# Weight sums moved from GpSimd to VectorE, and a last quarter that begins four runs early, in a two-layer encoder

## What is computed

```python
for i in range(2):
    h = rms_norm(x, mix_norm[i])
    x = x + (neighbourhood_attention(h, ...) if i == 0 else sliding_window_gqa(h, ...))
    h = rms_norm(x, mlp_norm[i])
    x = x + square(relu(h @ mlp_w_in[i])) @ mlp_w_out[i]
return rms_norm(x, final_norm)
```

## Time and profile before

| | us |
|---|---|
| median of 3 runs | 1118.18 (1117.50 to 1118.21) |
| the profiled execution's own time | 1117.47 |
| its span, first to last instruction | 1115.8 |
| PE busy | 1091.5 (98%) |
| DVE busy | 885.5 (79%) |
| ACT busy | 596.0 (53%) |
| POOL busy | 272.7 (24%) |

### The profile page before, as it was taken

One profiled execution on the slowest core, in us unless ns is written; L12 is line 12 of the kernel. 1 busy time (PEld: TensorE's weight loads), 2 busy tenths in 40 slices (PEclk: granted clock), 3 DMA queues, 4 the chain that ended last, 5 costly groups with the idle time before them and its releaser, 6 DMA issues.

```text
span 1115.8 us, 18152 instructions
## 1 busy us (share of the span) xinstructions
PE 1091.5 (98%) x6524; PEld 961.5 (86%) x6524; DVE 885.5 (79%) x1432; ACT 596.0 (53%) x1020; POOL 272.7 (24%) x340
## 2 busy tenths in 40 slices
PE   8999999999999999999889999999999999999987
PEld 6888888888998998998887888888899899899786
DVE  7778887768958968968887799976895895895795
ACT  6777767555425425425444788845543542542553
POOL 6544332200210210210464244201020030020151
PEclk9999999999999999999999999999999999999999
DMA  6332322232332332332213233234313313313312
GB/s 213 115 91 78 108 79 75 88 121 94 114 114 76 113 114 76 114 114 71 100 58 105 56 97 100 71 104 132 124 48 133 124 46 133 119 53 132 101 51 76
DMA packets 37098, 109.65 MB, mean 98 GB/s; under 512 B 6480, under 2 KB 10864, under 8 KB 37024
## 3 DMA queue, kind: packets, MB, share of 16 engines
q1 hardware_dynamic: 32112, 100.74, 26.9%
q0 software_dynamic: 4768, 7.90, 2.9%
q10 hardware_dynamic: 144, 0.02, 0.0%
HBM read 105.93 MB, written 2.70 MB: 97 GB/s over the span
## 4 chain that ended last, share of the span: by engine, by line
PE 93%; DVE 3%; issue 1%; ACT 1%; POOL 0%; DMA 0%; DVEq 0%; POOLq 0%; ACTq 0%
PE acc L661 17%; PE acc L663 17%; PE acc L662 17%; PE pt_ps L661 4%; PE pt_ps L663 4%; PE pt_ps L662 4%; PE acc L695 3%; PE s_ps L661 3%; PE s_ps L663 3%; PE s_ps L662 3%; PE om_ps L661 2%; PE om_ps L662 2%; PE om_ps L663 2%; PE om_ps L987 2%; PE pt_ps L974 2%; PE om_ps L814 1%
## 5 line engine op out<-in xcount | busy, mean ns | idle before, releaser
L661 PE MATMUL acc<-h_hi,w_parts 128*128 128x512 f32 x736 | 291.3, 396 | 2.5 <-DVE w_parts L1473 2.0
L663 PE MATMUL acc<-h_hi,w_parts 128*128 128x512 f32 x736 | 286.8, 390 | 0.0
L662 PE MATMUL acc<-h_lo,w_parts 128*128 128x512 f32 x736 | 286.6, 389 | 0.0
L661 PEld LDWEIGHTS acc<-h_hi,w_parts 128*128 128x128 f32 x736 | 138.3, 188 | 33.1 <-DVE w_parts L1473 2.8
L663 PEld LDWEIGHTS acc<-h_hi,w_parts 128*128 128x128 f32 x736 | 138.1, 188 | 29.4
L662 PEld LDWEIGHTS acc<-h_lo,w_parts 128*128 128x128 f32 x736 | 138.4, 188 | 28.1 <-issue 0.7
L1267 ACT CAST w_parts<-w_raw 128x1024 fp32r<-128x1024 f32 x62 | 65.3, 1054 | 144.3 <-PE acc L663 120.8
L661 PE MATMUL pt_ps<-u_hi,w_parts 128*128 128x256 f32 x384 | 110.5, 288 | 5.7 <-DVE x_res L1741 3.5
L1293 ACT CAST w_parts<-room 128x1024 fp32r<-128x1024 f32 x64 | 66.0, 1046 | 87.9 <-DVE room L1695 67.4
L663 PE MATMUL pt_ps<-u_hi,w_parts 128*128 128x256 f32 x384 | 109.4, 285 | 0.0
L662 PE MATMUL pt_ps<-u_lo,w_parts 128*128 128x256 f32 x384 | 109.4, 285 | 0.0
(11 more groups left out here) (201 smaller groups left out, 2557.8 us busy)
## 6 DMA issues: line engine op xcount, KB each, us to landing
w_raw<-in_wstream SPq DMA_DIRECT2D x148, 512.0 KB, 3.6
d_raw<-in_wstream SPq DMA_DIRECT2D x32, 512.0 KB, 5.1
room<-rpb_reversed POOLq DMA_DIRECT2D x64, 62.0 KB, 2.4
room<-t_shifted POOLq DMA_DIRECT2D x64, 48.0 KB, 2.1
x_res<-in_xT SPq DMA_DIRECT2D x8, 256.0 KB, 5.6
room<-inverse_sums SPq DMA_DIRECT2D x16, 128.0 KB, 3.2
out_y<-x_res SPq DMA_DIRECT2D x7, 256.0 KB, 2.5
inverse_sums<-sw_turned SPq DMA_DIRECT2D x32, 1.0 KB
```

What stands on the lines that cost most here:

```text
L661: nc.tensor.matmul(dst, a[0], b[0], start=start, stop=False, skip_group_check=resumed)
L662: nc.tensor.matmul(dst, a[0], b[1], start=False, stop=False, skip_group_check=resumed)
L663: return nc.tensor.matmul(dst, a[1], b[0], start=False, stop=stop, skip_group_check=resumed)
```

## The change

**Weight sums.** DVE makes all four sums of a group (`weight_sum`, n = 1 to 4); POOL makes none, and keeps only the additions of `first_run` (`add_first_runs`). In a cycle slot 0 now has s1, s3, s2, and slot 1 piece 1 and s4. In the last quarter s1 of group 1 is made ahead of the last pair's `hidden_sums`.

**Pieces.** Piece 3 is now a22 (128x512), piece 4 (s3, s4). `WEIGHTS_PIECE` follows: run 4 needs piece 3, runs 7 and 3 piece 4.

**Early runs.** In the last quarter the order begins 1, 2, 6, 5, 7, and PE first does the k-steps 0 to 2 of runs 1, 6, 5 and 2 of group 0, and then the last k-step of each, as the last pair's parts come. Run 2 no longer goes on in run 1's bank: it gets the bank that run 1 of group 1 uses (`apart`), so (1,1) waits for the take of (0,2), and DVE takes run 1 in two additions.

**Squares.** ACT writes the square of tile 0 into `sqsum` itself and those of tiles 1 to 7 each into a place of its own (`square_at`), without waiting for a sum. DVE adds them, and for m = 0 makes the low parts, in the last cycle (`finish_tiles`) and behind it. `sqsum` is no longer cleared ahead of these norms.

**SW.** In `two_after_norm` chunk 0 takes its k-steps 6 and 7 ahead of k-steps 3 to 7 of chunk 1, with `statistics` ahead of its last.

```diff
-WEIGHTS_PIECE = {1: 1, 2: 1, 5: 2, 6: 2, 7: 3, 3: 3, 4: 4}
+WEIGHTS_PIECE = {1: 1, 2: 1, 5: 2, 6: 2, 4: 3, 7: 4, 3: 4}
@@ run_order
+    if q == QUARTERS - 1:
+        order = [(0, 1), (0, 2), (0, 6), (0, 5), (0, 7)]
@@
+def apart(m, q, g, r):
+    return (q, g, r) == (3, 0, 2) or (m, q, g, r) == (1, 3, 3, 3)
@@ GpSimd
-            def first_sums(m, q, g):
...
-            def add_square(n, k):
...
+            def add_first_runs(m):
+                for g in range(GROUPS):
...
+                    nc.gpsimd.tensor_tensor(at, at, once[:, None, :].to_broadcast([P, 2, FEW]), ALU.add).then_inc(first_added, 1)
+                    pool.wait_ge(run_taken, RUN[4 * m + 3, g, 6])
+                    nc.gpsimd.tensor_tensor(x_quarter(g, 0, 1), x_quarter(g, 0, 1), once, ALU.add).then_inc(first_added, 1)
@@ TensorE, run
+                    elif apart(m, q, g, r):
+                        pe.wait_ge(run_taken, RUN[quarter, g - 1, 2] if g else RUN[quarter - 1, GROUPS - 1, 2])
+                    elif q == QUARTERS - 1 and (g, r) == (1, 1):
+                        pe.wait_ge(run_taken, RUN[quarter, 0, 2])
@@ TensorE, mlp
+                    if ends:
+                        for r in (1, 6, 5, 2):
+                            run(m, q, 0, r, range(PAIRS_K - 1))
@@ TensorE, two_after_norm
-                for k in range(6):
+                for k in range(3):
                     part(c + 1, g + 1, h_tile, [k])
-                    if k == 2:
-                        statistics(n)
                 for k in range(6, KT):
                     pe.wait_ge(h_low, KT * n + k + 1)
+                    if k == KT - 1:
+                        statistics(n)
                     part(c, g, h_tile, [k])
+                for k in range(3, KT):
                     part(c + 1, g + 1, h_tile, [k])
@@ VectorE
+            def weight_sum(m, q, g, n):
...
+                if n == 1:
...
+                    nc.vector.tensor_tensor(s1, a21, a22, ALU.add).then_inc(sums_made, 1)
+                elif n == 3:
...
+                    nc.vector.tensor_tensor(s3, a11, a21, ALU.subtract).then_inc(sums_made, 1)
...
+            def prepare_group(m, q, g, cycle, slot):
+                if slot == 0:
+                    if q < QUARTERS - 1 or g > 1:
+                        weight_sum(m, q, g, 1)
+                    weight_sum(m, q, g, 3)
+                    weight_sum(m, q, g, 2)
+                elif slot == 1:
+                    group_low(m, q, g, 1)
+                    weight_sum(m, q, g, 4)
+                elif slot == 2:
+                    group_low(m, q, g, 2)
+                elif slot == (4 if cycle else 3):
+                    group_low(m, q, g, 3)
+                elif slot == (5 if cycle else 4):
+                    group_low(m, q, g, 4)
...
+            def finish_tiles(m, slot):
+                if slot in (0, 2, 4):
+                    add_square(m, 1 + slot // 2)
+                elif slot in (6, 7):
+                    add_square(m, slot - 2)
+                if m == 0:
+                    if slot < 4:
+                        finish_h(2, slot)
+                    elif slot > 6:
+                        finish_h(2, slot - 3)
@@ VectorE, mlp, behind take_run(m, q, g, r)
-                        if ends and cycle and m == 1 and slot in (5, 6):
-                            finish_x(4, At(2 * cycle - 2 + slot - 5))
+                        if ends and cycle == GROUPS - 1:
+                            finish_tiles(m, slot)
```

## The result

The changed kernel takes **1121.42 us** (median; 1121.23 to 1123.31), the kernel before 1118.18; the ratio is 1.0033, 95% interval 1.0023 to 1.0042. It is slower, where I forecast 1.5 us faster, and it lies outside the range of 1113.5 to 1119.3. Executions of one kernel spread by 1 to 4 us, so the medians and intervals count, and a profile shows where the time lies in one execution. The profiled executions have spans of 1119.7 and 1115.8 us.

The account below looks back on a forecast made before the run. DVE was taken to pace PE in cycle 0 of the last quarters. 3.2 won in layer 0, less 0.3 (SW), 0.1 (layer 1) and 1.3 (first statistic), gave 1.5 won: 1116.7 us, own range 1115.4 to 1117.8, wider range 1113.5 to 1119.3.

Parts of the forecast that it names:

- the upper bound: Price of POOL's first addition between DVE's low part and s4: bounds 0.76 and 1.3 us, 1.24 taken.
- rival A: POOL doesn't cut in between low part and s4, or costs 0.76 beside a take: 1114.1 us, chance 0.22.
- SW: SW chunks: `statistics` stands 0.7 later, less 0.36; 0.3 us lost, a wait of 2.2 instead of 1.87.
- The first statistic: End of layer 1: the sixth square stands behind run (3,5)'s additions, statistic at 1103.8 instead of 1102.51, 1.3 us lost.
- DVE paces PE in cycle 0: Last quarter's entry: DVE's queue up to the take of (0,7) sets when (0,4) starts, not the 2.6 us waits.
- PE is through with (0,7) at 543.6: Layer 0's last quarter: PE finishes (0,7), then stands 3.1 us ahead of (1,1) for the take of (0,2).
- PE has 1.4 + 1.2 to spare there: At (1,1): the 3.1 us wait drops the clock, but PE's slack absorbs a slow stretch, which costs 1.3 elsewhere.
- Rival D: Clock falls in a new wait, paid in SW and ahead of the last run: 1118.0 to 1119.3 us, chance 0.11.
- Rival C: DVE becomes the bound of the whole last quarter, POOL costing 2.8 us a cycle: 1121.9 us, chance 0.12.
- Layer 0's gain of 2.0 + 1.3 with its slow stretch: Layer 0, cycle 2: (2,7) starts at 566.6 without a wait, 2.0 us won; the slow stretch of 1.3 goes too.
- 0.2 for (0,4) in each layer: Last quarter's entry: (0,4) begins at 551.0 instead of 551.20, 0.2 us won in each layer.
- 0.1 lost at (2,7) of layer 1: Layer 1, cycle 2: (2,7) begins at 566.6 instead of 566.5 on layer 0's scale, 0.1 us lost.

Follow-up runs that it names:

- s4_later: three_undone with group 1's fourth weight sum in the last quarters behind DVE's take of (0,6), not ahead of it: 1110.88 us, ratio 0.9941.
- no_early: The changed kernel without the early k-steps, last quarters in the order of before, run 2 again in run 1's bank: 1117.45 us, ratio 0.9991.
- take6_first: The changed kernel with DVE's take of (0,6) ahead of that of (0,2) in the last quarters: 1118.69 us, ratio 1.0002.
- take6_squares_sw: take6_first with layer 1's fourth and fifth added squares one place earlier and the SW chunks in the order of before: 1115.54 us, ratio 0.9981.
- three_undone: no_early with layer 1's fourth and fifth added squares one place earlier and the SW chunks in the order of before: 1112.59 us, ratio 0.9955.
- take6_filled: take6_first with eight more useless k-steps in run (0,5) of both last quarters, in the wait ahead of (0,7): 1116.14 us, ratio 0.9989.
- squares_ahead: The changed kernel with layer 1's fourth and fifth added squares one place earlier in DVE's queue: 1119.63 us, ratio 1.0014.
- pool_one_column: The changed kernel with POOL's eight pairs of first-run additions cut to one column each, the rest left out: 1119.69 us, ratio 1.0014.
- sw_undone: The changed kernel with the first two SW chunks in the order of before: 1121.0 us, ratio 1.0022.

## Why the prediction was wrong

**What held.** PE waits 0.41 for the last hidden part (forecast 0.5). POOL gets in between the low part and s4: s4 at 1.75 (forecast 1.9), a price of 1.07 where I took 1.24, nearer to the upper bound; so rival A falls. My nearest row, the step at 286.91, had shown 1.1, and 1.24 stood on no row. (The ten runs that I took for the length of one are 14.6 and not 14.5, which changes nothing: in s4_later (0,7) takes 1.44.) The Trainium skill ("SBUF — State Buffer", on the shared port pair) states that one engine gets the pair for a whole instruction and the other fully blocks. The trace agrees with it: s4 takes 1.75 beside POOL's addition and 0.68 where that is cut to 2 columns. SW: a wait of 1.90 against 1.72, 0.2 lost where I had 0.3. The first statistic: 1.3 lost in waiting, as worked out, behind both additions of (3,5). "DVE paces PE in cycle 0" held for the kernels without early k-steps: in no_early a half clock at the entry of one layer moved nothing, and in s4_later (0,4) waits 1.02 for DVE. It didn't hold for the changed kernel, where (0,4) waits for nothing.

**The step that failed** is "PE is through with (0,7) at 543.6". I let PE run through (0,7) and then stand 3.1 ahead of (1,1) for the take of (0,2). But (0,7) itself waits, for the take of (0,6). My own working had that take on DVE behind the take of (0,2) and a low part; I didn't ask who waits for it. Before, (0,6) was taken second and PE had two more runs, (0,5) and (0,2), to do ahead of (0,7). With the early k-steps only one k-step of each of the first four runs is left, and PE stands at (0,7) from 541.97, where before it began it at 546.15. What comes then is a chain and no longer an overlap: the take of (0,6), and behind it three whole runs of PE, (0,7), (1,1) and (1,6), ahead of (0,4). The forecast of DVE's queue was near: the take of (0,7) ends 15.5 us after the first run, 0.77 of it in standing for PE, where I had 15.0. But PE is only through with its three runs at 17.8 (18.4 in layer 1), where I had (0,4) at 15.1. Against take6_first, (2,7) of layer 1 comes 2.1 later: 1.5 of it stands at (0,7) already (12.12 against 10.66), and 0.6 comes behind it, in a longer stretch at half the clock.

**The second step** is the clock, "PE has 1.4 + 1.2 to spare there". I priced the half clock of the long wait at nothing, because it had been free in layer 0 before. It was free there because DVE was the later of the two at that place. Here PE is, so nothing is to spare, and (0,7) at 2.70 is on the path. The filling prices it: 0.7 and 0.5 against take6_first, and 1.4 in each layer against take6_squares_sw. Rival D had the mechanism, in SW's wait and at the end too, with the cost of 1.3 right in the profile of the changed kernel for SW and near it at the end (1.4), where no_early lost 2.9; it counted the fall at the entry as free.

**Rival C** gave 1121.9, next to the measured time, by luck, for a reason that isn't there: PE waits for no take in cycles 1 to 3, and the same DVE work without the early k-steps gives the fastest kernels. A number that comes out right says nothing of its mechanism.

**The terms that were too small.** Layer 0's gain of 2.0 + 1.3 with its slow stretch was there once the early k-steps were gone: three_undone has (2,7) 2.9 earlier and 1.7 more up to the next last quarter. I had 0.2 for (0,4) in each layer, and by no_early the sums on DVE alone give 0.6; I had 0.1 lost at (2,7) of layer 1, and they win 0.7. The early k-steps, from which the 0.2 was to come, cost 3 (three_undone against take6_squares_sw).

By these parts: sums and squares on DVE, with the order of before otherwise and the squares in time, −5.0 (ratio 0.9955); early k-steps in a good order of the takes +3; their order of takes as it was made +2.7; the place of the squares +1.8; SW +0.4. That is 2.9 in sum, against the 3.2 to 3.7 that the medians and the ratio give; by the ratios the parts come to 4.7. SW's part isn't clear of the noise. The parts share the clock, so they need not add exactly.

## What to carry to other kernels

When work is pulled ahead of a wait, list for each instruction behind it what it waits for, and redo that list in the new order: the next one in the same bank inherits the wait. Where another engine sets the pace, starting early gathers several short waits into one long one; that wins nothing, and costs what the clock loses behind it. Take the order of the takes from who waits for each, and put the last input of a statistic well ahead of it: one wait of 1.45 at the end cost its length once more in the changed kernel and twice more in no_early.

## What the runs showed of the hardware

Filling two waits of 3.7 us with 2.9 us each of useless matmuls made the program 1.5 to 2.5 us faster (by the ratios and by the medians). At the entries, where the granted clock stayed at 1.00, it gave 1.2 us in sum. The same kind of wait doesn't always bring the fall. The wait of 2.36 at the entry of the last quarter was followed by half the clock in layer 1 of three_undone (columns as above, clock third from the end),

```profile
1056.00:1061.00 5.00, 4.76 (x27) 4.76 (x28) 4.82 (x8) 3.40 (x4) 1.19 (x1) 0.66 0.06 25
```

and not in layer 0 of s4_later:

```profile
538.00:543.00 5.00, 3.77 (x29) 3.56 (x30) 4.79 (x9) 2.83 (x3) 0.51 (x1) 1.00 0.21 84
```

A wait of 1.90 in SW brought it in the changed kernel and in take6_first and not in take6_filled, squares_ahead, pool_one_column and no_early. What decides stays open. The changed kernel, squares_ahead and sw_undone are alike up to (2,7) of layer 0 and wait 0.4 and 5.54 there, and yet (2,7) comes at 32.2, 33.0 and 33.2; so one profile isn't enough to price a wait. POOL's addition of 2 columns took 1.10 beside DVE's low part of 1.22 and 0.57 (at 572.62) beside a DVE sum of 0.68, and ended 0.05 behind it each time: the length of a POOL instruction in the trace can hold standing, and isn't its work alone.
